# Attention stage: prompt blocks start 20 page steps later than before

## The reference, cut to what matters

```python
def forget_attend(q, q_idx, k, v, fk, fq):
    s = jnp.einsum('bqhd,bkhd->bhqk', q, k, preferred_element_type=jnp.float32) * (HEAD_DIM ** -0.5)
    s = s + (jnp.transpose(fq, (0, 2, 1))[..., :, None] - jnp.transpose(fk, (0, 2, 1))[..., None, :])
    mask = jnp.arange(k.shape[1])[None, :] <= q_idx[:, None]
    s = jnp.where(mask, s, NEG)
    p = jax.nn.softmax(s, axis=-1)
    return jnp.einsum('bhqk,bkhd->bqhd', p.astype(v.dtype), v)
...
            if past is None:
                o = prompt_attend(q, k_all, v_all, F_all)      # prompt: blocks of 128 queries
            else:
                o = forget_attend(q, n_past + jnp.arange(n), k_all, v_all, F_all, F_all[:, n_past:])
            o = o.reshape(bsz, n, W_B).astype(h.dtype)
            out = (o * jax.nn.silu(zg)) @ b_out_w[j]
```

## Time and profile before

| what | value |
|---|---|
| median of 3 runs | 2052.34 us (2045.05 to 2061.64) |
| profiled execution: its time / the span in the trace | 2060.06 us / 2058.3 us |
| granted TensorE clock over the span | 0.946 |
| busy share of the span: PE, PEld, DVE, ACT, POOL | 89%, 72%, 41%, 25%, 32% |
| DMA, mean over the span | 167 GB/s |
| attention stage, about | 1297 to 1915 us of the span |

### The profile page before, as it was taken

One profiled execution on the slowest core, in us unless ns is written; L12 is line 12 of the kernel. 1 busy time (PEld: TensorE's weight loads), 2 busy tenths in 40 slices (PEclk: granted clock), 3 DMA queues, 4 the chain that ended last, 5 costly groups with the idle time before them and its releaser, 6 DMA issues. The chain is left out here.

```text
span 2058.3 us, 31546 instructions
## 1 busy us (share of the span) xinstructions
PE 1824.9 (89%) x12403; PEld 1480.3 (72%) x12403; DVE 851.8 (41%) x1204; ACT 516.2 (25%) x992; POOL 666.8 (32%) x545
## 2 busy tenths in 40 slices
PE   3899799989979899399999999499999999997686
PEld 1899799979967676199999999366565555563464
DVE  2731414407225668512110000566666666662344
ACT  2210101101012222210000010155555554552111
POOL 0523223223238778122222232311111111110475
PEclk9999899999989999599999999699999999998799
DMA  9223223231155544134333331568888988878653
GB/s 309 83 83 118 66 96 116 88 106 59 50 195 194 171 144 147 43 89 129 107 86 90 93 97 64 182 201 274 305 298 308 308 310 289 283 259 283 216 199 133
DMA packets 209342, 343.23 MB, mean 167 GB/s; under 512 B 40985, under 2 KB 141962, under 8 KB 206387
## 3 DMA queue, kind: packets, MB, share of 16 engines
q1 hardware_dynamic: 176204, 290.25, 42.9%
q10 hardware_dynamic: 32991, 50.95, 7.1%
HBM read 295.52 MB, written 45.63 MB: 166 GB/s over the span
## 5 line engine op out<-in xcount | busy, mean ns | idle before, releaser
L136 PE MATMUL ps<-actH,w_hi_a 128*128 128x352 f32 x912 | 201.3, 329 | 20.1 <-POOL w_lo_a L124 20.1
L136 PE MATMUL ps<-actH,w_lo_a 128*128 128x352 f32 x912 | 197.9, 325 | 0.0
L136 PE MATMUL ps<-actL,w_hi_a 128*128 128x352 f32 x912 | 197.6, 325 | 0.0
L1038 PE MATMUL ps<-w_hi_t,actH 128*128 128x512 f32 (+1 forms) x432 | 145.8, 420 | 57.7 <-DVE actL L1109 30.5
L136 PE MATMUL ps<-actH,w_hi_c 128*128 128x352 f32 x792 | 173.3, 327 | 15.8 <-DVE w_lo_c L94 15.8
L111 POOL TENSOR_TENSOR w_lo_t<-w_raw_t,w_hi_t 128x1024 fp32r<-128x1024 f32 x70 | 183.8, 2626 | 5.6
L136 PEld LDWEIGHTS ps<-actH,w_hi_a 128*128 128x128 f32 x912 | 155.8, 191 | 33.8 <-issue 33.8
L122 POOL CAST w_hi_a<-w_raw_a 128x1024 fp32r<-128x1024 f32 (+1 forms) x48 | 45.1, 939 | 398.3 <-PE ps L136 282.6
L136 PE MATMUL ps<-actH,w_lo_c 128*128 128x352 f32 x792 | 171.2, 324 | 0.0
L136 PE MATMUL ps<-actL,w_hi_c 128*128 128x352 f32 x792 | 171.0, 324 | 0.0
L1574 POOL TENSOR_SCALAR diag<-ident,rinv 128x128 f32<-128x128 f32 x128 | 75.6, 602 | 286.9 <-DVE rinv L1850 286.7
(11 more groups left out here) (215 smaller groups left out, 2875.5 us busy)
## 6 DMA issues: line engine op xcount, KB each, us to landing
K<-in_cache_k_dram SPq DMA_DIRECT2D x128, 512.0 KB, 5.9
V<-in_cache_v_dram SPq DMA_DIRECT2D x128, 512.0 KB, 4.9
w_raw_t<-in_a_out_w_dram SPq DMA_DIRECT2D x48, 512.0 KB, 3.6
ada<-in_ada_w_dram SPq DMA_DIRECT2D x16, 1024.0 KB, 6.3
w_raw_a<-in_a_in_w_dram SPq DMA_DIRECT2D x32, 512.0 KB, 4.4
w_raw_t<-in_b_out_w_dram SPq DMA_DIRECT2D x24, 512.0 KB, 3.7
g_d<-g ACTq DMA_DIRECT2D x16, 528.0 KB, 2.7
mov_t<-g_d SPq DMA_DIRECT2D x16, 528.0 KB, 4.5
```

The lines of the kernel that those rows point to most:

```text
L136: mm = pe.matmul(acc[:, c, 0:CH], wt[:, j % SPL, k, :], act[:, k0 + k, c * CH:(c + 1) * CH], start=first and k == 0 and s == 0, stop=last ...
L1038: mm = pe.matmul(ps[0:rows_of(t), 2 * (n % 4) + c, :], act[:, k, at], wt[:, c * BANK:(c + 1) * BANK], start=k == 0 and s == 0, stop=k == n ...
```

## The change

Prompt rounds start `PL` = 20 steps later: round R now stands in steps 20 + 4R to 23 + 4R. Its scores still run two rounds ahead, from step 14. What stood ahead of the loop for rounds 0 and 1 is gone from there, and the loop's conditions admit it instead (`0 <= R + 1 < RN`, `0 <= R + 2 < RN`). `STEPS` stays 151. Loads of a pair of heads move by 20 steps, and pair 0 is in the list like the others; the first B moves from 1.0 to 3.2. Waits that stood ahead of PE's loop move to where their data is first needed. The diff, cut (the same replacement of `R < RN` by `now` or by `0 <=` conditions recurs in ACT's and DVE's loops):

```diff
+        PL = UN + 4
...
-        for p in range(1, NP):
+        for p in range(NP):
             for n, what in enumerate(("q", "k", "nF0", "nF1", "Vt", "z")):
-                loads.append((UN * p - 20 + 2 * n, what, p))
+                loads.append((PL + UN * p - 20 + 2 * n, what, p))
         for bq in range(NB):
-            loads.append((UN * bq - 8 if bq else 1.0, "B", bq))
+            loads.append((UN * bq - 8 if bq else 3.2, "B", bq))
...
-                query_load(0, "q")
-                query_load(0, "k")
-                forget_load(0, 0)
-                forget_load(0, 1)
-                gate_load(0)
-                value_load(0)
...
-                pe.wait_ge(s_LT, 1)
-                for R, c in ((0, 0), (0, 1), (0, 2), (1, 0), (1, 1)):
-                    scores(R, c)
-                pe.wait_ge(s_qst, 4)
-                pe.wait_ge(s_set, 64)
-                pe.wait_ge(s_ones, 6)
                 for s in range(STEPS):
-                    R, k = s // 4, s % 4
+                    R, k = (s - PL) // 4, (s - PL) % 4
+                    now = 0 <= R < RN
...
-                    if R + 2 < RN and k >= 2:
+                    if 0 <= R + 2 < RN and k >= 2:
                         scores(R + 2, k - 2)
...
-                for u, h in ((LONG, 0), (LONG, 1), (SHORT, 0), (SHORT, 1)):
-                    exps(0, u, h)
...
-                    if 0 <= r < NP and s % UN == 2:
-                        act.wait_ge(s_gate, 4 * (r + 1))
-                        act.dma_start(og_d[r, :, 0:SEQ], ogp[:, r % 2]).then_inc(s_ogd[r % 2], 16)
+                    if 0 <= p < NP and (s - PL) % UN == 1:
+                        act.wait_ge(s_gate, 4 * (p + 1))
+                        act.dma_start(og_d[p, :, 0:SEQ], ogp[:, p % 2]).then_inc(s_ogd[p % 2], 16)
...
-                for c in range(3):
-                    logits(0, c)
-                    if c:
-                        row_max(0, c - 1)
-                logits(1, 0)
-                logits(1, 1)
```

More of the change, by code:

```diff
@@ L1641, in norms @@
                     pe.wait_ge(s_diag, 4 * R + 4)
+                    if R == 0:
+                        pe.wait_ge(s_ones, 6)
                     for u in (LONG, SHORT):
@@ L1665, in page_scores @@
                         pe.wait_ge(s_rowe, j)
+                    else:
+                        pe.wait_ge(s_LT, 1)
+                        pe.wait_ge(s_qst, 4)
                     for c in range(NP // HG):
@@ L1696, in side @@
                     if what == "score":
+                        if r == 0:
+                            pe.wait_ge(s_set, 64)
                         for c in range(NP // HG):
@@ L1726, in _ @@
                         turn_K(s)
-                    if R < RN and k < 3:
+                    if now and k < 3:
                         turn_probs(R, k, 0)
-                    if R + 1 < RN and k == 1:
+                    if 0 <= R + 1 < RN and k == 1:
                         scores(R + 1, 2)
-                    if R + 2 < RN and k >= 2:
+                    if 0 <= R + 2 < RN and k >= 2:
                         scores(R + 2, k - 2)
@@ L1738, in _ @@
                         page_scores(s // KG - 1)
-                    if R < RN and k < 3:
+                    if now and k < 3:
                         turn_probs(R, k, 1)
-                    if R < RN and k:
+                    if now and k:
                         values(R, k - 1)
-                    if R < RN and k == 3:
+                    if now and k == 3:
                         norms(R)
@@ L1767, in probs_out @@
                     act.copy(PT[:, n % 2, h, 0:w * P], ps[:, 2, 0:w * P]).then_inc(s_PTe, 1)
-                for u, h in ((LONG, 0), (LONG, 1), (SHORT, 0), (SHORT, 1)):
-                    exps(0, u, h)
                 for s in range(STEPS):
-                    R, k = s // 4, s % 4
+                    R, k = (s - PL) // 4, (s - PL) % 4
+                    now, p = 0 <= R < RN, (s - PL) // UN - 1
                     r, work = s // UN - 1, side_work(s)
@@ L1789, in _ @@
                         act.copy(PTn[:, :], ps[0:NS, 6, 0:P]).then_inc(s_side_read, 1)
-                    if R + 1 < RN and k in (1, 2):
+                    if 0 <= R + 1 < RN and k in (1, 2):
                         exps(R + 1, LONG, k - 1)
-                    if R < RN and k < 3:
+                    if now and k < 3:
                         probs_out(R, k, 1)
-                    if R + 1 < RN and k == 3:
+                    if 0 <= R + 1 < RN and k == 3:
                         exps(R + 1, SHORT, 0)
@@ L1910, in _ @@
                 link(dve, dve.tensor_scalar(nmask[:, :], nmask[:, :], 1.0, -NEG, ALU.subtract, ALU.mult))
-                invert(0, LONG)
                 for s in range(STEPS):
-                    R, k = s // 4, s % 4
+                    R, k = (s - PL) // 4, (s - PL) % 4
                     r, work = s // UN - 1, side_work(s)
@@ L1921, in _ @@
                                         ps[:, 7, :].rearrange("p (c n) -> p c n", c=4)).then_inc(s_Kd, 1)
-                    if R < RN and k == 0:
+                    if 0 <= R < RN and k == 0:
                         invert(R, SHORT)
-                        if R + 1 < RN:
-                            row_max(R + 1, LONG)
+                    if 0 <= R + 1 < RN and k == 0:
+                        row_max(R + 1, LONG)
                     if work:
@@ L1947, in _ @@
                         gate(R - 1)
-                    if R + 1 < RN and k == 2:
+                    if 0 <= R + 1 < RN and k == 2:
                         row_max(R + 1, SHORT)
-                    if R + 1 < RN and k == 3:
+                    if 0 <= R + 1 < RN and k == 3:
                         invert(R + 1, LONG)
```

## The result

The changed kernel takes 2080.15 us (median of 4 runs, 2078.84 to 2081.28), the kernel before 2053.67 in the same comparison. The ratio is 1.0118 with a 95% interval of 1.009 to 1.0147: slower by 24 us by the ratio and 26 us by the medians. The forecast was 2064 us with a range of 2029 to 2090. The time lies in the range and the kernel is slower as forecast, but the loss is about twice the forecast's 11.7 us.

What follows compares the result with a forecast made beforehand. PE was taken to bound the middle, and loads the last V pages. Terms -26 (front), +4 and +12 (middle), +20.7 (end), +1 (last stores) sum to +11.7 us: 2064 us against the 2052.34 median, range 2029 to 2090.

Steps and rivals of the forecast that it cites:

- Middle, loads: Steps 22 to 127: Vt right behind B makes K pages late, 2 us for each of six B loads: +12 us.
- the upper bound ("some 20"): Steps 22 to 127: load lateness costs some 20 us if each wait also lowers PE's clock for a page step.
- Rival 1: Middle: B with Vt behind it bounds each 16-step period, 4 us a period, 2082 us; chance 0.18.
- the likeliest case: Whole kernel: the sum as it stands, within 1% either way, own range 2040 to 2073 us; chance 0.53.
- Front: Start to step 22: less work ahead of the loop, then lone K pages; step 22 comes earlier, -26 us.
- Rival 2: Front: lone K pages never get the full clock, 2076 us; chance 0.30 together with Rival 1.
- End: Steps 128 to 147: each holds a V page and a prompt step, 57.7 us against 37.0: +20.7 us.
- the last stores: After the last page: the last pair's result is stored beside the samples' result: +1 us (0 to 3).
- Middle, PE's work: Steps 120 to 127: short before, full after the change, 33.5 us against 29.7: +4 us.
- Rival 3: Middle: late K pages go away and the front keeps -36, 2024 us; chance 0.17 together with smaller gains.

Runs made afterwards that it cites:

- e2: Kernel before the change, with only each pair's Vt load moved to right behind bias load B: 2072.47 us, ratio 1.0104.
- e9: Changed kernel, with only each pair's Vt load moved four steps after B, so B stands alone: 2064.12 us, ratio 1.0064.
- e3: Changed kernel, with B's four DMAs issued one step apart and away from Vt: 2045.43 us, ratio 0.9952.
- e4: Kernel before the change, with B's four DMAs issued one step apart: 2041.53 us, ratio 0.9948.
- e5: e3 plus idle transposes on PE behind the first K pages, so PE does not stand still at the front: 2044.50 us, ratio 0.9956.
- e11: Changed kernel, with G stored four times so B, still whole, reads 16 separate rows instead of 4 repeated: 2062.04 us, ratio 1.0032.

## Why the prediction was right or wrong

**Middle, loads: the term that was too small.** The forecast saw the place and the mechanism (Vt behind B, six waits, three pages of lead), and e2, e9 and e3 show them. It priced them at 12 us as 2 us of lateness in each of six periods. The middle lost 24.8, of which 4 are the full steps, so the term was 20.8. Of this 13.7 us are waits (25.1 against 11.4, 2.3 a period), near the 12 forecast, and the other 7 came with the clock: PE's busy time in the middle rose by 12.5 us, and only by 4.9 from e4 to e3, where the clock is 1.00 in both. The forecast named this clock as the upper bound ("some 20") and left it out of the sum. Its own row had shown the cost: the earlier trace rows has transposes of 1.48 us behind a wait of 3.07. With waits of 4.2 us on average, this happened behind five of six. Rival 1 had 4 us a period and 2082 us, and is the case that came true: 3.5 us a period and 2080.15 us. The forecast gave it 0.18, and a loss of over 1% 0.30; the likeliest case, within 1%, had 0.53 and didn't come by the ratio (1.0118, interval from 1.009), and its own range of 2040 to 2073 was missed. The range held because it was drawn past the rivals. Rival 1's name for the load, the bound of each period, is too strong: DMA is busy for 0.83 of the middle, and for 0.89 in e3, where the middle is 30.9 us shorter.

**Front.** DVE's first K copy came at 1313.56, 22.2 us after PE's first instruction of the stage, which is the forecast's 1319.4 on the trace of before (22.4). Step 14 was forecast 67 us into the stage and came at 71.1, step 22 at 93 and 97.5. The four late us are in the lone pages: half clock in pages 1 to 4 was assumed, but pages 6 to 8 and 11 and 12 ran at it too, and the two waits for loads were 4.7 and 6.3 us where 2 and 6 had been put; the first page scores won some of it back (2.42 us, not 3.84). Rival 2 was half right (0.79 granted over the front, and 0.63 up to page 9), and e5 suggests why it would have cost little alone: with B in pieces, the loads set the end of this part.

**End.** 60.6 us against 57.7 forecast, with the clock at 1.00. The waits for the probability copy are 5.7 us in ten pieces, where 4.5 was put in as 0.9 a round; a late bias adds 1.1 more. The steps themselves were priced about right, from starts on PE: no K page, no page scores, 2.79 us left. No part made up for another: the front missed by 4.4 us, the middle by 8.8 and the end by 3.0, all in one direction, and only the last stores by 1.3 in the other.

**Middle, PE's work, and the last stores.** Steps 120 to 127 took 33.7 us, forecast 33.5. The stage's end didn't move (forecast +1): the pair's store was issued at 1931.39, the samples' at 1933.21, and the next stage loads at 1936.55, 5.2 us after the last V page.

Rival 3, that the late pages of the middle go away, didn't come by the shift but by other means: with B in pieces it is worth 11 to 13 us to the kernel before and 34 to 35 to the changed one. In its sum stands 18 us for the end where the forecast has 20.7; the text gives no reason for that, and it decides nothing.

## What to carry to other kernels

A move of work by whole steps moves its loads too; look at what the new order of the queue puts right behind its slowest transfer, and count the lead of the buffers behind it in time, not in pages. Moving work to where loads bound the time pays only as far as something is won for it: 20 steps won 21.6 us at the front and cost 23.7 at the end, while 8 steps, enough to clear the start, with the bias in four pieces won 19.7 at the front against e4 and cost about 8 at the end. That version has the lowest median here (2030.52 us, ratio 0.9895; the interval of 12 steps overlaps). A shift by 20 with the bias whole is slower than none, and with the bias in pieces in both it is no gain. A wait on PE should be priced with the lower clock that can follow it: in these traces waits of 3.07 and 4.51 us were followed by transposes of 1.48 and 1.94 us, but one of 3.48 us, behind the last sample's bias, by transposes of 1.06.

## What the hardware showed that was not expected

The issue of a load can itself hold its engine: behind B and Vt the K load's instruction on SP took 1.84 us in the period shown, where the K load before it took 0.33, and 0.36 behind B and Vt in e11. And PE's clock stayed at half with small gaps: transposes of 1.94 us with waits of 0.88 us between them kept that length through pages 1 to 4, for 10.4 us, and the clock rose within the unbroken page scores behind them (2.42 us, where they take 1.92 at the full clock).

Repeating rows in a load's source showed in its packets: four at a time from four repeated rows, up to 16 from 16 separate rows of the same bytes. The separate rows took 0.75 us a packet instead of 0.44, and B became only some 30% shorter.
